# A gated delta rule layer on one core: the first merge level in four column groups, and the last unit in another order

## The reference

```
mod = silu(c) @ ada_w + ada_b ; shift, scale, gate = split(mod)
h = rms_norm(x, norm_w) * (1 + scale) + shift
q, k, v, z, b, a = split(h @ w_in)
q, k, v = silu(causal_conv4(q, k, v)) ; q = l2_norm(q) / sqrt(128) ; k = l2_norm(k)
beta = sigmoid(b) ; g = -exp(a_log) * softplus(a + dt_bias)
per head and token:  S = exp(g) (I - beta k k^T) S + beta k v^T ; o = S^T q
y = (rms_norm(o) * silu(z)) @ w_out
out = rms_norm(x + gate * y) * final_norm_w
```

## Time and profile before

| | us |
|---|---|
| Median of 3 runs (lowest, highest) | 1124.75 (1124.22, 1125.43) |
| The profiled execution, its time | 1122.74 |
| The profiled execution, span of its trace | 1120.9 |
| PE busy | 1054.8 (94%) |
| DVE busy | 788.5 (70%) |
| ACT busy | 509.4 (45%) |
| POOL busy | 528.3 (47%) |

### The profile page before, as it was taken

How to read it: one execution, slowest core, us unless ns; L and a number is a source line. 1 busy time by engine, 2 the same in 40 slices (tenths; PEclk the granted TensorE clock), 3 DMA queues, 4 the chain that set the end, 5 groups by cost and what they waited for, 6 DMA issues and landing times.

```text
span 1120.9 us, 19408 instructions
## 1 busy us (share of the span) xinstructions
PE 1054.8 (94%) x5628; PEld 854.4 (76%) x5628; DVE 788.5 (70%) x1696; ACT 509.4 (45%) x1262; POOL 528.3 (47%) x750
## 2 busy tenths in 40 slices
PE   3897799999999999999999999999999999999984
PEld 2766587878878787878878787888878787888853
DVE  4778586785858586695858686695768686695845
ACT  4663434444444434445354534435353544435333
POOL 2242544546344743546444753446444753456413
PEclk9899999999999999999999999999999999999998
DMA  9922231224121231223221221223222222213013
GB/s 317 314 87 70 67 79 49 58 60 105 42 67 40 82 82 45 60 58 87 58 67 40 75 73 53 67 58 86 50 62 55 75 69 55 69 54 90 22 40 130
DMA packets 142055, 87.30 MB, mean 78 GB/s; under 512 B 21254, under 2 KB 136616, under 8 KB 141992
## 3 DMA queue, kind: packets, MB, share of 16 engines
q1 hardware_dynamic: 141992, 86.68, 27.6%
HBM read 77.76 MB, written 8.91 MB: 77 GB/s over the span
## 4 chain that ended last, share of the span: by engine, by line
PE 81%; DVE 10%; issue 4%; ACT 2%; POOL 1%; DMA 1%; SPq 0%; DVEq 0%; POOLq 0%; ACTq 0%
PE bank L415 40%; PE bank L525 16%; DVE work L976 3%; PE bank L569 3%; PE bank L557 2%; PE bank L579 2%; PE bank L582 2%; PE bank L561 2%; PE bank L607 2%; DVE y L999 2%; PE bank L494 1%; PE bank L430 1%; PE bank L463 1%; PE bank L510 1%; PE bank L437 1%
## 5 line engine op out<-in xcount | busy, mean ns | idle before, releaser
L1399 POOL TENSOR_TENSOR w_lo<-w_raw,w_hi 128x256 fp32r<-128x256 f32 x384 | 306.5, 829 | 258.6 <-ACT w_hi L704 258.6
L415 PE MATMUL bank<-h_hi,w_hi 128*128 128x512 f32 x760 | 332.3, 437 | 4.6 <-ACT w_hi L704 4.6
L415 PE MATMUL bank<-h_lo,w_hi 128*128 128x512 f32 x760 | 300.3, 395 | 0.0
L415 PE MATMUL bank<-h_hi,w_lo 128*128 128x512 f32 x760 | 203.8, 400 | 0.0
L976 DVE SCALAR_TENSOR_TENSOR work<-pre,cw,work 128x512 f32<-128x512 f32 x192 | 170.5, 888 | 9.6 <-DVE work L976 2.1
L415 PEld LDWEIGHTS bank<-h_hi,w_hi 128*128 128x128 f32 x760 | 143.9, 189 | 38.1 <-ACT w_hi L704 5.2
L415 PEld LDWEIGHTS bank<-h_lo,w_hi 128*128 128x128 f32 x760 | 144.2, 190 | 30.7 <-issue 3.8
L415 PEld LDWEIGHTS bank<-h_hi,w_lo 128*128 128x128 f32 x760 | 142.9, 188 | 31.1 <-issue 1.0
L1442 POOL TENSOR_TENSOR og_lo<-work,og_hi 128x256 fp32r<-128x256 f32 x64 | 47.2, 738 | 216.9 <-ACT og_hi L786 216.9
L525 PE MATMUL bank<-wo_hi,og_hi 128*128 128x512 f32 x256 | 113.5, 443 | 7.1 <-DVE y L999 7.1
L999 DVE SCALAR_TENSOR_TENSOR y<-bank,o_rs,y 128x512 f32<-128x512 f32 x128 | 89.9, 744 | 24.6 <-PE bank L525 23.9
(11 more groups left out here) (181 smaller groups left out, 1702.5 us busy)
## 6 DMA issues: line engine op xcount, KB each, us to landing
w_raw<-in_gdn_w_in SPq DMA_DIRECT2D x96, 512.0 KB, 4.0
work<-in_ada_w SPq DMA_DIRECT2D x8, 1024.0 KB, 9.6
w_raw<-in_gdn_w_out SPq DMA_DIRECT2D x16, 512.0 KB, 3.3
y<-in_x SPq DMA_DIRECT2D x8, 512.0 KB, 9.1
work<-in_ada_w SPq DMA_DIRECT2D x8, 512.0 KB, 5.7
n_dram<-work SPq DMA_DIRECT2D x16, 256.0 KB, 2.3
out<-y SPq DMA_DIRECT2D x8, 512.0 KB, 2.6
work<-in_ada_b SPq DMA_DIRECT2D x1, 512.0 KB, 5.4
```

The source lines that it names most:

```text
L415: mm = nc.tensor.matmul(bank[m % 2][:, :], w[:, m % 2, k, :], h[:, k, half, :], start=(r == 0), stop=(r == MM - 1))
L1399: i = nc.gpsimd.tensor_tensor(w_lo[:, k % 2, j:j + 2, :], w_raw_k[:, k % 2, j:j + 2, :], w_hi[:, k % 2, j:j + 2, :].bitcast(F32), ALU.subt ...
```

## The change

At level 0 of the merge each matmul of 128 weight columns becomes four of 32, one for each column group of the array (rows 0, 32, 64 and 96 of the bank). In `merge_p` each takes only the 16 moving columns of its own block, and `merge_p_out` reads the 16 columns of each chunk four times under the mask. In `merge_d` each takes all 64 moving columns. In both groups 4 matmuls become 16.

In the last unit: the fillers follow a table of their own, `FILL_LAST`, which spreads the 48 matmuls to the end of chunk 0; chunks 1 and 3 use banks 0 and 1 and parts of w_hi and w_lo in place of banks 6 and 7, og_hi and og_lo, and wait for one chunk less of y; the squares, roots and norms of tiles 0 to 4 move ahead; the gate of z (`silu(u, 0)` and `silu(u, 1)`) and ScalarE's evacuation of the second z tile move behind; `gate_o(3)` moves ahead of additions; `add_y(3)` stands before `norm_y(5)`; the last tile is normed and stored in two halves. All of the diff, with one line of context:

```diff
@@ line 256 of the kernel before @@
         FILLS = (((12, 12), (10, 14), (6, 2)), 16, ((8, 8, 6), (8, 8, 6), (2, 2, 6), (2, 2, 6)), 8)
+        FILL_LAST = (((6, 6), (6, 6), (4, 4)), 6, ((4, 4, 2), (0, 0, 0), (0, 0, 0), (0, 0, 0)), 0)
         FILL_FIRST = (((6, 4), (6, 4), (2, 2)), 0, FILLS[2], FILLS[3])
...
         BASE_STEPS = (((), (0, 8), (8, 11), (11, 15), ()), ((0, 3), (6, 9), (9, 11), (11, 15), (3, 6)))
+
+        def out_bank(c, n, last):
+            return bank[n] if last and c % 2 else bank[6 + n]
+
+        def gated_hi(c, last):
+            return w_hi[:, 0, 0:2, :] if last and c % 2 else og_hi[:, :, :]
+
+        def gated_lo(c, last):
+            return w_lo[:, 0, 0:2, :] if last and c % 2 else og_lo[:, :, :]
@@ line 389 of the kernel before @@
                          ).then_inc(fw_in, 16)
-            for t in range(TILES):
+            for t in range(TILES - 1):
                 sp.wait_ge(fin_done, t + 1)
                 sp.dma_start(out_v[:, t, :], y[:, t, :]).then_inc(stored[t % 2], 16)
-            for i in range(2):
-                sp.wait_ge(stored[i], 16 * TILES // 2)
+            for j in range(2):
+                sp.wait_ge(fin_done, TILES + j)
+                cols = slice(j * HALF, (j + 1) * HALF)
+                sp.dma_start(out_v[:, TILES - 1, cols], y[:, TILES - 1, cols]).then_inc(stored[j], 16)
+            sp.wait_ge(stored[0], 16 * (TILES // 2 + 1))
+            sp.wait_ge(stored[1], 16 * (TILES // 2))
@@ line 470 of the kernel before @@
                     passed(pe, "t_turned", u, lv)
-                p_bank = halves(bank[5], lv, (lv % 2) * DV)
                 for c in range(NCH):
                     if lv == 0:
-                        mm = nc.tensor.matmul(p_bank[:, c, :, :], nmat[:, c, :], pairs(tm, lv)[:, c, :, 0, :],
-                                              start=True, stop=True)
+                        for b in range(0, P, 32):
+                            mm = nc.tensor.matmul(bank[5][b:b + 32, c * BLK:(c + 1) * BLK], nmat[:, c, b:b + 32],
+                                                  tm[:, c, b:b + BLK], start=True, stop=True)
                     elif lv == 1:
@@ line 491 of the kernel before @@
                     if lv == 0:
-                        mm = nc.tensor.matmul(halves(bank[4], lv)[:, c, :, :], pm[:, lv, c, :], u_odd,
-                                              start=True, stop=True)
+                        for b in range(0, P, 32):
+                            mm = nc.tensor.matmul(halves(bank[4], lv)[b:b + 32, c, :, :], pm[:, lv, c, b:b + 32], u_odd,
+                                                  start=True, stop=True)
                     elif lv == 1:
@@ line 517 of the kernel before @@
                         passed(pe, ("kdec_done", "n_done")[n], u + 1, 1)
+                last = not ahead
                 if n == 0:
                     passed(pe, "og_lo_done", u, c + 1)
-                    passed(pe, "y_added", u, c)
+                    passed(pe, "y_added", u, max(c - 1, 0) if last else c)
+                    if last and c == 1:
+                        passed(pe, "evacuated", u, 2)
+                hi, lo = gated_hi(c, last), gated_lo(c, last)
                 for m in range(2):
-                    for q, (a, w) in enumerate(((og_hi, wo_hi), (og_hi, wo_lo), (og_lo, wo_hi))):
-                        mm = nc.tensor.matmul(bank[6 + n][:, :], a[:, m, :], w[:, m, n * 512:(n + 1) * 512],
+                    for q, (a, w) in enumerate(((hi, wo_hi), (hi, wo_lo), (lo, wo_hi))):
+                        mm = nc.tensor.matmul(out_bank(c, n, last)[:, :], a[:, m, :], w[:, m, n * 512:(n + 1) * 512],
                                               start=(m == 0 and q == 0), stop=(m == 1 and q == 2))
@@ line 691 of the kernel before @@
                 body(hd + 1, 0)
-            body(HEADS - 1, 1, last=True)
+            body(HEADS - 1, 1, last=True, fills=FILL_LAST)
@@ line 780 of the kernel before @@
-            def og_high(u, c):
+            def og_high(u, c, last):
                 passed(act, "og_done", u, c + 1)
-                passed(act, "out_done", u, c)
-                nc.scalar.activation(og_hi[:, :, :], og, ACT.Copy).then_inc(S["og_hi_done"], 1)
+                passed(act, "out_done", u, max(c - 1, 0) if last else c)
+                nc.scalar.activation(gated_hi(c, last), og, ACT.Copy).then_inc(S["og_hi_done"], 1)
@@ line 828 of the kernel before @@
                 if last:
+                    square_y(0)
+                    square_y(1)
+                    square_y(2)
                     evacuate_z(u, 0, 0)
-                    evacuate_z(u, 1, 1)
                 else:
@@ line 856 of the kernel before @@
                     if c > 0:
-                        og_high(u, c - 1)
+                        og_high(u, c - 1, last)
                     if not last and c == 3:
@@ line 870 of the kernel before @@
                         tanh(u, 4, 2, cvv[:, 0, :])
-                    if last:
-                        square_y(c)
-                og_high(u, NCH - 1)
+                    if last and c == 0:
+                        evacuate_z(u, 1, 1)
+                    if last and c == 1:
+                        square_y(3)
+                    elif last and c == 3:
+                        square_y(4)
+                og_high(u, NCH - 1, last)
@@ line 954 of the kernel before @@
             body(HEADS - 1, 1, last=True)
-            for t in range(4, TILES):
+            for t in range(5, TILES):
                 square_y(t)
@@ line 986 of the kernel before @@
                 passed(dve, "og_lo_done", u, c)
+                if isinstance(u, int) and u == LAST:
+                    passed(dve, "silu_done", u, 2)
                 for m in range(2):
...
-            def add_y(u, par, c):
+            def add_y(u, par, c, last):
                 passed(dve, "out_done", u, c + 1)
...
                     yt = y_v[:, par, c, n * 512:(n + 1) * 512]
-                    i = stt(out=yt, in0=bank[6 + n][:, :], scalar=o_rs[:, c:c + 1], in1=yt, op0=ALU.mult, op1=ALU.add)
+                    i = stt(out=yt, in0=out_bank(c, n, last)[:, :], scalar=o_rs[:, c:c + 1], in1=yt, op0=ALU.mult, op1=ALU.add)
                 i.then_inc(S["y_added"], 1)
@@ line 1075 of the kernel before @@
                 mask = pair_mask[:, lv // 2, :].rearrange("p (b q w) -> p b q w", q=2, w=w)[:, :, 0, :]
-                nc.vector.tensor_tensor(p_out, halves(bank[5], lv, (lv % 2) * DV),
-                                        mask.unsqueeze(1).to_broadcast([P, NCH, nb, w]), ALU.mult
+                p_in = halves(bank[5], lv) if lv == 2 else bank[5][:, 0:NCH * w].rearrange(
+                    "p (c w) -> p c w", c=NCH).unsqueeze(2).to_broadcast([P, NCH, nb, w])
+                nc.vector.tensor_tensor(p_out, p_in, mask.unsqueeze(1).to_broadcast([P, NCH, nb, w]), ALU.mult
                                         ).then_inc(S["merge_p_out"], 1)
@@ line 1106 of the kernel before @@
                 dve.wait_ge(fin_pow, t + 1)
-                stt(out=y[:, t, :], in0=y[:, t, :], scalar=frs[:, t:t + 1], in1=w_raw[:, 0, :],
-                    op0=ALU.mult, op1=ALU.mult).then_inc(fin_done, 1)
+                for j in range(0, D_MODEL, D_MODEL if t < TILES - 1 else HALF):
+                    cols = slice(j, D_MODEL if t < TILES - 1 else j + HALF)
+                    stt(out=y[:, t, cols], in0=y[:, t, cols], scalar=frs[:, t:t + 1], in1=w_raw[:, 0, cols],
+                        op0=ALU.mult, op1=ALU.mult).then_inc(fin_done, 1)
@@ line 1136 of the kernel before @@
                 merge_d_out(u, 1)
-                if last:
-                    silu(u, 0, zt[:, 0, :], gate=True)
-                else:
+                if not last:
                     silu(u, 0, cvk[:, other, :])
@@ line 1147 of the kernel before @@
                 merge_d_out(u, 2)
+                if last:
+                    silu(u, 0, zt[:, 0, :], gate=True)
+                    norm_y(0)
                 if par == 1 and not last:
@@ line 1159 of the kernel before @@
                         if last:
-                            silu(u, 1, zt[:, 1, :], gate=True)
+                            norm_y(1)
                         else:
...
                                 make_n(u + 1, other)
+                    elif last and c == 1:
+                        silu(u, 1, zt[:, 1, :], gate=True)
                     elif last:
-                        norm_y(c - 1)
+                        norm_y(c)
                     if not last:
@@ line 1184 of the kernel before @@
                                             ).then_inc(S["o_done"], 1)
+                    if last and c == 3:
+                        gate_o(u, 3)
                     if c >= 2:
-                        add_y(u, par, c - 2)
+                        add_y(u, par, c - 2, last)
+                    if last and c == 3:
+                        norm_y(4)
                     if not last:
```

(30 more changed lines are left out.)

## The result

| | us |
|---|---|
| Median before, beside it | 1125.09 (1124.22 to 1125.69, 4 runs) |
| Median after | 1109.34 (1107.77 to 1110.00, 4 runs) |
| Ratio, 95% interval | 0.986 (0.984 to 0.988) |
| Profiled execution of after, span | 1107.77, 1106.0 |
| PE, DVE, ACT, POOL busy | 1047.4, 788.9, 509.8, 531.4 |

The forecast was 1109.3, for the profiled execution 1107.2. In the traces the span fell by 14.9 us: 10.94 in the last unit (from its first merge matmul to the end of the span, 60.77 to 49.83), 4.8 in the fourteen loop units (888.84 to 884.05), and 0.8 was lost ahead of unit 1 (its first merge matmul at 171.32, then 172.16).

A forecast was written before the change was run, and what follows sets the result against it. TensorE's busy time bounds the loop, chains of waits the last unit. Savings of 6.2 and 9.3 us, 15.5 in all, take the profiled 1122.74 to 1107.2; with 2.0 more the median is 1109.3, range 1106 to 1112.

The forecast's parts named there:

- First group 0.58: First merge level, first product: four overlapping column groups cost 0.58 us, a gain of 0.32.
- two at a time: Rival for the first merge level: no more than two column groups overlap, 1114.0 us; chance 0.14.
- one stream: Rival for the first merge level: loads overlap but moving columns go one after another, 1117.8 us; chance 0.12.
- the slower one: Rival for the first merge level: column groups take turns, at least 1.43 us each, 1130 us in all; chance 0.07.
- Second group 0.58: First merge level, second product: 64 moving columns hide under the weight step, so 0.58 us, a gain of 0.32.
- An odd unit keeps 0.35: Odd loop units: pm on VectorE leaves 0.03 of the first group's gain, the second's 0.32 stays; 0.35 us kept.
- An even unit keeps 0.53: Even loop units: VectorE's chain can come earlier only by its 0.53 us of idle time, so 0.53 is kept.
- Unit 0: nothing: Unit 0, ahead of the loop units: it waits for other things, so no gain was counted.
- Last unit, 9.3: The last unit: shorter chains of waits save 9.3 us in sum, with bounds of 6 and 11.
- (a): Last unit, up to the first state product: with fewer early fillers it comes at 1075.3 instead of 1078.84, gain 3.5 us.
- (f): Last out-projection: waits only for og_lo, held up about 1 us, so it starts at 1099.7; gain so far 6.6 us.
- (h): Norms behind the last addition: two take 2.4 us, the last norm's halves run 1107.6 to 1108.9; gain so far 8.9.

The follow-up runs named there:

- e4: The changed kernel with the first merge level's loops over chunks and column groups swapped, so each group gets its matmuls in a row; 1120.01 us, ratio 0.9967.
- e3: The changed kernel with 16 instead of 64 moving columns per column group in the first level's second product, for timing only; 1108.15 us, ratio 0.9863.
- e7: The changed kernel with each even unit's last addition to y moved behind VectorE's first mask and small q step of the next unit; 1108.20 us, ratio 0.9846.
- e6: The changed kernel with VectorE's gating of w_out's second half moved behind the SiLU that follows the level 1 subtraction; 1115.96 us, ratio 0.9915.
- e1: The kernel before with only the first merge level in four column groups, the last unit untouched; 1119.57 us, ratio 0.9963.
- e5: The changed kernel itself, timed again as the measure for later runs; 1109.85 us, ratio 0.9855.
- e10: The changed kernel with the old filler table in the last unit, all 48 spent before the chunks; 1111.09 us, ratio 0.9873.
- e11: The changed kernel with one pair of banks and one og_hi and og_lo in the last unit, as before; 1116.02 us, ratio 0.9914.
- e2: The kernel before with only the last unit's edits, keeping the old first merge level; 1113.39 us, ratio 0.9904.

## Why the prediction was right, step by step

- *First group 0.58.* Measured 0.57, with 32 starts within 0.27. The column groups are independent in loads and matmuls (the 32 loads start within 0.23, each 0.11 long); both rivals of Part 1 (two at a time, one stream) and the slower one (in turn) fell. What e4 adds: this holds as long as neighbours in the queue are of different groups.
- *Second group 0.58.* Mis-sized: 0.78. The step that failed is "64 columns are 0.029, under the 0.035 of the weights: hidden". With 16 columns it is 0.57 (e3), so the columns are not hidden; inside a group the step is 0.056 with 64 and 0.032 with 16, also where one group runs alone (e4). Whether they pass at half the rate or behind the weights stays open.
- *An odd unit keeps 0.35.* Measured 0.34 (means 63.40 to 63.06), but made up otherwise. From the first group to the second it kept 0.14 (3.72 to 3.58) where 0.03 was forecast; that the group is tied to pm behind VectorE's pause was right (e7 takes the tie away, and the distance is 3.32). From the second group to level 1 it kept 0.29 (3.83 to 3.54). Of this 0.20 stands in even units too (3.73 to 3.53). The rest was a hold inside before's second group, which I had not read: its second record started 0.16 after the first (936.89, 937.05) and not 0.06, in units where pm is written only just before. Behind the merge 0.09 was lost again (45.77 to 45.86), and I can't say to what. The number was hit by errors that cancel.
- *An even unit keeps 0.53.* Measured 0.34 (63.57 to 63.23). Right that VectorE's chain bounds it (e3: a shorter second group brings nothing; e6: the wait goes with the gating). Wrong that the chain can come forward by its whole idle time: 0.20 of it came back as a wait for ScalarE's evacuation. The two groups passed 0.55 faster (7.40 to 6.85), TensorE's wait for the transpose took 0.14 of that back, and 0.07 went behind the merge (45.62 to 45.69). So 4.8 in the loop and not 6.2.
- *Unit 0: nothing.* The first group's gain was indeed hidden there: TensorE waits for w_hi behind it, 1.06 before and 1.72 after. But the term put at nothing was a loss: the period grew by 1.75 (63.26 to 65.01), and by 2.2 to 2.6 in the other traces with the four groups interleaved and unit 0's order untouched (e1, e3, e5, e10, e11). Only 0.8 of it shows ahead of unit 1 because unit 0 happened to start 0.9 earlier in after (108.06, then 107.15). In all eleven traces with the four groups interleaved the period is 65.0 or more; in the three without (before, e2, e4) it is 63.3 to 63.9. In all of the eleven VectorE waits for the transfer of w_out, in none of the three; here e1:

```profile
118.11 1.23 DVE L1044 TENSOR_TENSOR w_raw<-w_raw,gate_bc 128x1024 f32<-128x1024 f32 x1 [2.14 <-DMA w_raw<-in_gdn_w_out]
```

  There the first half of w_out landed 3.4 after its issue and the second 5.3, in before 3.8 and 3.2. The second took 4.2 to 5.4 in the eleven and 3.1 to 3.5 in the three. A second thing parts the same traces, and I had not looked at it: the granted clock over unit 0 is 0.95 in the three and 0.88 to 0.92 in the eleven. Unit 0 in before and in after (TensorE, its loads, VectorE, ScalarE, POOL, then the clock):

```profile
108.06:171.32 63.26, 55.77 (x290) 44.60 (x291) 42.69 (x97) 28.43 (x72) 30.74 (x44) 0.95 0.25 67
107.15:172.16 65.01, 57.01 (x338) 44.59 (x338) 42.49 (x97) 28.46 (x72) 30.76 (x44) 0.89 0.25 64
```

  No run parts the transfer from the clock, and why either changes is open.
- *Last unit, 9.3.* Measured 10.94. (a) The first state product came 15.1 in, as forecast (the terms printed there add up to 1069.5 and not to the 1068.8 used: SiLU with subtract and transpose took 1.7 where 2.2 stand); e10 puts 2.5 of the gain on the fillers. (b) 4.57 for 4.5, (c) 3.72 for 3.9, (d) 5.64 for 5.6, (e) 0.87 for 0.87. (f) is the step that was off: the last out-projection was to be held up about 1 us for og_lo and was not; og_lo was written by 1094.40, and the last out-projection followed its predecessor without a gap (1094.64), 1.1 earlier than forecast. (Its gain of 1.5 also needs the end of a wait of 0.97 ahead of chunk 2's out-projection in before, which the text does not name.) (g) and (h) passed that on (the root beside a norm did take 1.17, as assumed), (i) the half stores landed 2.1 after their issue.
- The sum hit the median within 0.1, and that is luck: errors cancelled (1.4 less in the loop, 0.8 lost ahead of unit 1, 1.6 more in the last unit), the profiled execution was missed by 0.6 (1107.2 for 1107.77), and the four runs spread over 2.2. The price of the slowest rival, 1144, is 1143.3 by its own terms. A rule weighed there, a floor of 25 ns between matmul starts (the Trainium skill, TensorE: Matmul & The Clock Gate, "Wait — 56ns, not 53.3ns?"), fits what happens inside one column group (0.032 at the least here), and not across four (0.27 over 31 steps).

## What to carry to other kernels

Interleave column groups in program order, matmul by matmul; a loop over chunks inside a group made the loop units slower than the old matmuls of 128 columns (894.7 against 888.8). Price a 32-column matmul by its moving columns too. Before counting a gain in one engine, look at what the chained engine waits for further along: idle time ahead of its first step is not slack for the whole chain. Look at the units outside the loop too, and at their clock: a term put at nothing there lost 1.75 us. And when an instruction is moved, look through every wait that counts it or its kind: the moves tried here had their price in ScalarE's order, in unit 0 and at the squares of y.

## What the runs showed of the hardware that was not expected

Thirty-two small matmuls in four column groups start 0.009 apart on average, while each group keeps 0.032. At each of the six returns of the loop to its start VectorE pauses for 1.6 to 1.8 us in which nothing in the trace releases it (both kernels); put where the engine would wait anyway (e7), the pause costs nothing: the odd unit without a return ahead of it and the six with one all take 62.8.
